# A hybrid mixer block on one core: scores a projection and a half apart, the next block's k projected behind them

## What is computed

```
h = rms_norm(x, ln_g);  proj = h @ w_in
scores = q @ k^T * 64**-0.5 + alibi, masked to the window of 128
p = softmax(concat(scores, sink))[:-1]
y_attn = (p @ v) * silu(g_attn)
```

## Time and profile before

| | us |
|---|---|
| median of 3 runs | 1454.54 |
| lowest, highest | 1451.94, 1455.07 |
| profiled execution, its own time | 1452.87 |
| its span, first to last instruction | 1450.7 |

### The profile page before, as it was taken

How to read it: one execution, slowest core, us unless ns; L and a number is a source line. 1 busy time by engine, 2 the same in 40 slices (tenths; PEclk the granted TensorE clock), 3 DMA queues, 4 the chain that set the end, 5 groups by cost and what they waited for, 6 DMA issues and landing times.

```text
span 1450.7 us, 20622 instructions
## 1 busy us (share of the span) xinstructions
PE 1363.4 (94%) x7070; PEld 1112.5 (77%) x7070; DVE 1170.9 (81%) x2365; ACT 549.3 (38%) x1421; POOL 504.8 (35%) x640
## 2 busy tenths in 40 slices
PE   6989898989989899876999999999999999999998
PEld 5867676767778687755888888888888888888886
DVE  4877768685868675554989999989899998888886
ACT  5746555555555554330221221121222243333332
POOL 5254545445354534552010010110101255555552
PEclk9999999999999999988999999999999999999999
DMA  9757482939384736657031230330326756545531
GB/s 214 218 125 263 124 284 89 288 110 268 124 254 153 203 146 162 245 130 222 12 131 54 108 131 24 136 130 14 131 88 250 286 193 213 164 158 163 159 126 73
DMA packets 112426, 230.78 MB, mean 159 GB/s; under 512 B 16464, under 2 KB 74192, under 8 KB 104656
## 3 DMA queue, kind: packets, MB, share of 16 engines
q1 hardware_dynamic: 88192, 205.85, 42.5%
q10 hardware_dynamic: 24144, 23.80, 6.8%
HBM read 131.05 MB, written 98.57 MB: 158 GB/s over the span
## 4 chain that ended last, share of the span: by engine, by line
PE 66%; DVE 14%; DMA 8%; ACT 5%; POOL 3%; issue 2%; SPq 1%; POOLq 0%; ACTq 0%; DVEq 0%
PE wide L346 12%; PE wide L347 12%; PE wide L348 12%; DMA xs<-in_x_dram 5%; PE pair L1239 3%; PE pair L1233 3%; PE pair L1234 3%; DVE m_tail L1994 3%; DVE a_rows L1038 2%; ACT a_rows L909 2%; PE wide L1233 2%; PE wide L1234 2%; PE turn L1202 2%; PE wide L1239 2%; PE turn L347 2%
## 5 line engine op out<-in xcount | busy, mean ns | idle before, releaser
L1994 DVE SCALAR_TENSOR_TENSOR m_tail<-m_tail,m_taps 128x512 f32<-128x512 f32 x480 | 338.5, 750 | 4.6
L1233 PE MATMUL pair<-xT,w_hi 128*128 128x512 f32 x384 | 154.5, 402 | 27.0 <-ACT xT L333 23.5
L845 POOL TENSOR_SCALAR a_rows<-a_rows,a_inv 128x128 f32<-128x128 f32 x256 | 108.4, 443 | 204.1 <-DVE a_inv L1058 204.0
L1736 POOL TENSOR_TENSOR operand_sums<-m_y 128x512 f32<-128x512 f32 x75 | 102.2, 1362 | 167.7 <-PE wide L348 116.6
L108 POOL TENSOR_TENSOR pool_carrier<-pool_carrier 128x1 f32<-128x1 f32 x23 | 14.0, 611 | 394.5 <-DVE m_meanvar L2003 394.5
L1234 PE MATMUL pair<-xT,w_lo 128*128 128x512 f32 x384 | 150.8, 393 | 0.0
L1239 PE MATMUL pair<-xT,w_hi 128*128 128x512 f32 x384 | 149.2, 394 | 0.9 <-DVE xT L339 0.7
L346 PE MATMUL wide<-x_first,w_hi 128*128 128x512 f32 x320 | 125.4, 392 | 0.0
L346 PE MATMUL wide<-xT,w_hi 128*128 128x512 f32 x320 | 125.2, 391 | 0.0
L348 PE MATMUL wide<-x_first,w_hi 128*128 128x512 f32 x320 | 124.6, 389 | 0.0
L348 PE MATMUL wide<-xT,w_hi 128*128 128x512 f32 x320 | 124.5, 389 | 0.0
(11 more groups left out here) (262 smaller groups left out, 3233.8 us busy)
## 6 DMA issues: line engine op xcount, KB each, us to landing
xT_scratch<-xT SPq DMA_DIRECT2D x16, 2048.0 KB, 10.3
p_scratch<-a_rows SPq DMA_DIRECT2D x32, 512.0 KB, 2.6
x_first<-xT_scratch SPq DMA_DIRECT2D x16, 1024.0 KB, 8.7
xT<-xT_scratch SPq DMA_DIRECT2D x16, 1024.0 KB, 9.0
combo_scratch<-stage SPq DMA_DIRECT2D x28, 512.0 KB, 5.3
m_y<-y_scratch ACTq DMA_DIRECT2D x14, 1024.0 KB, 6.6
xs<-in_x_dram SPq DMA_DIRECT2D x20, 512.0 KB, 10.7
a_pT<-p_scratch SPq DMA_DIRECT2D x64, 128.0 KB, 4.7
```

What stands on the lines that cost most here:

```text
L845: last = nc.gpsimd.tensor_scalar(probs[b][:, h], probs[b][:, h], inv[:, b, h:h + 1], 0.5, ALU.mult, ALU.mult)
L1233: nc.tensor.matmul(out, w.hi(c)[:, kk, cols], st.hi[:, kk, :], start=(kk == 0), stop=False)
L1736: nc.gpsimd.tensor_tensor(operand_sums[:, i, 1], y_block(q, left), y_block(q, right), SIGN[op]).then_inc(operand_sum, 1)
L1994: nc.vector.scalar_tensor_tensor(out=conv[:, i, :], in0=h[:, i, j:j + TB], scalar=taps[:, i, j:j + 1], in1=conv[:, i, :], op0=ALU.mult, op ...
```

## The change

- PE: k of block n+1 is projected at the end of block n, behind g3. attend(n-1, 0) comes first in the block, then q0 to q3 with the fold in q3. scores(0) follows q3 directly, then attend(n-1, 1) and v. scores(1), with `turn_v` in it, stands in the middle of g0, scores(2) behind g1, scores(3) in the middle of g3.
- q0 and q1 wait for one kv less of the last scores.
- ACT: the four `scale` steps move out of the q projections, in between the exponentials; `take_v` and the copy of the transposed v are placed anew; the four early `split_hi` come before both exponentials of subtile 3.
- DVE: the four `turn_squares` move between the subtiles, all four early `split_lo` come before `take_scores(3)`; `square_more` comes after q_lo(1), `mean` before q_lo(3), `output(n-1, 0)` and the transpose of the last probabilities right after k_lo.
- POOL: the masks of subtiles 2 and 3 come before `root`, the mask of subtile 0 behind `normalise(1)`, that of subtile 1 behind `normalise(2)`.
- SP: the next x is loaded first; the load of subtile 2 comes before the store of subtile 3.
- The last block has an order of its own on each engine.

The diff:

```diff
@@ -739,10 +739,10 @@
...
             else:
+                st.load(sp, n + 1, (0, 1))
+                load_probs(sp, n - 1, 2)
                 store_probs(sp, n - 1, 3)
-                st.load(sp, n + 1, (0, 1))
-                for j in (2, 3):
-                    load_probs(sp, n - 1, j)
+                load_probs(sp, n - 1, 3)
@@ -860,18 +860,14 @@
             if n == 0:
                 make_seen()
             else:
-                mask(n - 1, 1)
+                for j in (2, 3):
+                    mask(n - 1, j)
             if n < NB - 1:
                 st.root(pool, n + 1, carrier)
-            if n > 0:
-                for j in (2, 3):
-                    mask(n - 1, j)
             for j in range(SUB):
                 normalise(n, j)
-                if j == 2:
-                    mask(n, 0)
-                    if n == NB - 1:
-                        mask(n, 1)
+                if j in (1, 2):
+                    mask(n, j - 1)
@@ -946,63 +942,70 @@
...
-            elif not final:
+            q_hi(n, 1)
+            if not first and not final:
                 st.square(act, n + 1)
-            q_hi(n, 1)
...
             q_hi(n, 2)
-            if not first and not final:
-                st.scale(act, n + 1, 0)
...
-            else:
-                st.scale(act, n + 1, 1)
             q_hi(n, 3)
-            if not first and not final:
-                st.scale(act, n + 1, 2)
-            for s in combos.of_block(n, (3,)):
+            for s in combos.of_block(n, (3, 4)):
...
-            if first:
-                for part in (0, 1):
-                    st.scale(act, 1, part)
-            act.wait_ge(st.squared, SUB + st.HALF * (n if final else n + 1))
-            copy_out(n, slot("v"), vT)
-            for s in combos.of_block(n, (4,)):
-                combos.split_hi(act, s)
-            if not first and not final:
...
+            if not final:
+                st.scale(act, n + 1, 0)
+            for kv in range(KV):
+                exps(n, 0, kv)
+            take_v()
+            if not final:
+                st.scale(act, n + 1, 1)
+            for kv in range(KV):
+                exps(n, 1, kv)
+            spread_v()
+            gate_tanh(n, 0)
+            if not final:
+                st.scale(act, n + 1, 2)
+                gate_tanh(n, 1)
+                exps(n, 2, 0)
+                exps(n, 2, 1)
                 st.scale(act, n + 1, 3)
-            if first:
-                st.scale(act, 1, 2)
-            for j in range(SUB):
...
-                if j == SUB - 1 and not final:
-                    for kk in range(st.AHEAD):
...
-                if final and j == 2:
-                    w.split_hi(act, CHUNK_GP)
-                if j:
...
-                if j == 0:
-                    gate_tanh(n, j)
...
-                if j == 0:
-                    act.wait_ge(v_turned, n + 1)
...
+                gate_tanh(n, 2)
+                for kk in range(st.AHEAD):
+                    st.split_hi(act, n + 1, kk)
+                exps(n, 3, 0)
+                gate_tanh(n, 3)
+                exps(n, 3, 1)
@@ -1108,69 +1111,84 @@
...
+            make_k_lo(n)
             if not first:
+                output(dve, n - 1, 0)
                 turn_squares_of_probs(SUB * n - 1)
-            make_k_lo(n)
             make_q_lo(n, 0)
...
-            if not first:
-                output(dve, n - 1, 0)
-                if not final:
-                    st.square_more(dve, n + 1)
...
-                if t == 1 and not first and not final:
+                if t == 3 and not final:
                     st.mean(dve, n + 1)
                 make_q_lo(n, t)
-                if t == 3 and not first and not final:
-                    st.turn_squares(dve, n + 1, 1)
+                if t == 1 and not first and not final:
+                    st.square_more(dve, n + 1)
                 make_combos(n, (t,) if t < 3 else (3, 4))
...
-                elif t == 2 and not final:
-                    st.turn_squares(dve, n + 1, 0)
-                elif t == 3 and first:
-                    for part in (0, 1):
-                        st.turn_squares(dve, 1, part)
-                elif t == 3 and not final:
-                    st.turn_squares(dve, n + 1, 2)
...
+            take_scores(n, 0, 0)
+            take_scores(n, 0, 1)
             if not first:
                 output(dve, n - 1, 1)
-            for j in range(SUB):
-                take_scores(n, j, 0)
-                if j in (1, 2):
...
-                take_scores(n, j, 1)
-                invert(4 * n + j, j % 2, 0)
-                if j == 3:
-                    turn_squares_of_probs(SUB * n + 2)
-                if first and j < 2:
-                    st.turn_squares(dve, 1, 2 + j)
-                elif j == 0 and not first and not final:
...
-                if j == SUB - 1 and not final:
-                    st.split_lo(dve, n + 1, 0)
-                if j:
-                    gate_make(n, j)
-                if j == SUB - 1 and not final:
-                    for kk in range(1, PIECE):
-                        st.split_lo(dve, n + 1, kk)
-                invert(4 * n + j, j % 2, 1)
-                if j == 0:
-                    gate_make(n, j)
-                if final and j == 2:
...
+            inverts(0)
+            next_x(0)
+            take_scores(n, 1, 0)
+            turn_squares_of_probs(SUB * n)
+            take_scores(n, 1, 1)
+            next_x(1)
+            inverts(1)
+            gate_make(n, 0)
+            if not final:
+                next_x(2)
+                gate_make(n, 1)
+                take_scores(n, 2, 0)
+                turn_squares_of_probs(SUB * n + 1)
+                take_scores(n, 2, 1)
+                inverts(2)
+                next_x(3)
+                gate_make(n, 2)
+                for kk in range(PIECE):
+                    st.split_lo(dve, n + 1, kk)
+                for kv in range(KV):
+                    take_scores(n, 3, kv)
+                turn_squares_of_probs(SUB * n + 2)
+                gate_make(n, 3)
+                inverts(3)
@@ -1220,7 +1238,7 @@
...
             if name[0] == "q":
-                need(pe, score_taken, 2 * SUB * n)
+                need(pe, score_taken, 2 * SUB * n - (1 if name in ("q0", "q1") and n > 0 else 0))
@@ -1283,36 +1301,48 @@
...
+        def halfway(action):
+
+            return lambda kk: action() if kk == KT // 2 - 1 else None
+
...
                 project(n, "k", lambda kk: st.transpose(pe, kk + TURNS) if kk + TURNS < KT else None)
-                project(n, "q0")
             else:
-                project(n, "k")
-                project(n, "q0")
                 attend(pe, n - 1, 0)
-            final = isinstance(n, int) and n == NB - 1
-            for name in ("q1", "q2", "q3", "v"):
-                project(n, name, folding(n) if name == ("q3" if first else "q2") and not final else None)
+            for name in ("q0", "q1", "q2", "q3"):
+                project(n, name, folding(n) if name == "q3" and not final else None)
             pe.wait_ge(q_taken, GROUP * (n + 1))
+            scores(n, 0)
             if not first:
                 attend(pe, n - 1, 1)
...
-            for j in range(SUB):
-                scores(n, j, turn_v if j == 1 else None)
-                project(n, f"g{j}")
+            project(n, "v")
             if final:
+                scores(n, 1, lambda: turn_v(n))
...
                 attend(pe, n, 0)
+            else:
+                project(n, "g0", halfway(lambda: scores(n, 1, lambda: turn_v(n))))
+                project(n, "g1")
+                scores(n, 2)
+                project(n, "g2")
+                project(n, "g3", halfway(lambda: scores(n, 3)))
+                project(n + 1, "k")
```

## The result

The changed kernel takes **1540.36 us** (median of 4 runs, 1538.24 to 1541.36) against 1454.8 (median of 4, 1451.94 to 1455.7). The ratio is **1.059**, 95% interval 1.0571 to 1.0608: 5.9% slower, +85.6 us. The forecast was 1498, with 1526 as the range's upper end, so the sign was right and the size was half of what came. The profiled execution has a span of 1537.9 us (before: 1450.7).

The account below looks back on a forecast made before the run. PE sets the pace, save where a DVE and ACT chain ends later. Middle blocks +6.1 six times (+36.6), block 0 +10.3, block 7 -3: +43.9 on 1452.87 gives 1496.8, median 1498 us; range 1460 to 1526.

Parts of the forecast that it names:

- A + 37.5: Fifth split_hi ready 37.5 us after the start of scores(1) (A = 0); PE wanted it at 26.8.
- The new wait at scores(0): PE waits some 2.2 us at each block's first scores until all of q3 is rounded, eight times.
- The front: Block's stretch from the end of k (T = 0) to the start of scores(1): 41.1 us in a middle block.
- I take 1.2: Delay of DVE's squares of the next x by the masks of subtile 3: 1.2 us, at most some 3.5.
- The tail: Block's stretch from the start of scores(1) to the end of the next k: 42.5 us.
- the upper end, 3.8: Most that the mask of subtile 1 could add to the four early split_lo; 2.0 us was taken.
- Block 0: First block: k ends at 105.5 against 95.2 before, +10.3 us.
- Block 7: Last block, no next x: scores(1) at 44 us after the end of k instead of 47.4; -3 us together.
- The third: Rival: squares and split_lo pay whole mask passes, 3.5 and 3.8 us; 87.7 a block, 1524 us; chance 0.18.
- The mild rival: POOL's masks miss the tail's DVE and ACT chain, squares are in time: 78.4 a block, 1463 us; chance 0.17.
- The faster rival: DVE's chain is hidden, fifth split_hi in time, PE loses only the q wait: 70.0 a block, 1403 us; chance 0.10.

Follow-up runs that it names:

- masks23_small: The changed kernel with GpSimd's mask passes of subtiles 2 and 3 cut to one head of eight (work left out): 1500.02 us, ratio 1.0322.
- masks01_small: The changed kernel with GpSimd's mask passes of subtiles 0 and 1 cut to one head of eight (work left out): 1502.17 us, ratio 1.0319.
- filler_all: The changed kernel with useless matmuls on PE: 40 ahead of k's fifth slice, 10 ahead of the fold, 8 ahead of the wait for q: 1520.76 us.
- filler_k: The changed kernel with 40 useless matmuls on PE ahead of the fifth slice of every k but the first: 1524.52 us, ratio 1.048.

## Why the prediction was right or wrong

**Direction: right**, by the mechanism named. PE waits for ACT's xT once a block, 10.5 us (forecast 8 to 10, some 60 in all; 72.6 measured; the sum itself had 37.5 - 26.8 = 10.7). The fifth split_hi is written at A + 38.3 (A = 155.89; 194.16 on ACT), forecast A + 37.5. The new wait at scores(0) is there eight times, 2.1 us in a middle block (forecast 2.2). negmax in take(2, 0) takes 1.03.

**The front, 41.1 forecast, 47.0 measured: wrong.** The step that failed is the squares, "I take 1.2". They start at T + 16.2 and end at T + 23.9, 4.9 us later than their 2.8 undisturbed, more than the 3.5 that I gave as the most: five squares met a pass; four lost 1.1 us each and the first 0.6. PE thus waited 3.2 at the fold, where the statement was that it waits under 2, and where the sum had 1.2. (That sum was loose in itself: it gave PE 1.3 to spare at the fold and still charged the squares' delay of 1.2 in full.) The second part of that step was never written: having cleared the fold, I priced no slow clock in the front at all, though the earlier trace rows showed it behind a wait of 2.7 us. It costs 3.4 a block, and is the larger part: of the 5.9 us missed, 3.4 are slow clock, 2.0 the wait and 0.5 the rest. With the squares in time (`masks23_small`) the front is 40.4, within the forecast's 39.9 to 41.1, so all the rest of that sum held.

**The tail, 42.5 forecast, 44.4 measured: the right mechanism, undersized.** The splits grew by 3.9, not 2.0: the upper end, 3.8, was the value to take. take(2, 0) grew by 0.9, not by 2.0, since only negmax met a pass. Behind the wait PE's 15 matmuls took 6.05 us instead of the 5.0 assumed: at 0.50 of the clock for 3.5 us, and the last of them not yet back at full. These are the stretches from 183.7 on:

```profile
183.70:194.20 10.50, 0.04 (x1) 0.00 (x0) 10.17 (x31) 4.44 (x21) 3.53 (x4) 0.59 0.04 15
194.20:197.70 3.50, 3.42 (x8) 2.75 (x9) 3.08 (x4) 1.87 (x4) 3.50 (x6) 0.50 0.25 104
```

**Block 0: +13.7, forecast +10.3.** The wait for q was 3.82 us there and the one of k 10.26. **Block 7: -6.7, forecast -3**: its scores(1) stand at T + 40.4 (694.18) and not T + 44, of which 2.4 are the masks that I expected it to wait 5.0 for, and which cost it 2.6; the other 1.2 I can't place:

```profile
685.57 1.09 PE L1220 MATMUL turn<-a_pT,a_v 128*64 128x128 f32 x16 [2.59 <-POOL a_rows L856]
...
753.96 1.97 PE L1220 MATMUL turn<-a_pT,a_v 128*64 128x128 f32 x16 [16.49 <-POOL a_rows L856]
```

In sum 13.7 + 79.7 - 6.7 = +86.7, of a span that grew by 87.2. Where block 1 stands for the six, 35 us of the missed time are the front's and 11 the tail's (the mean block is 0.6 us shorter than it), block 0 adds 3 and block 7 takes 4 off.

**The rivals.** The third (full blocking, 1524) came nearest, and its mechanism is what happened; it fell short by the front's slow clock, 3.4 a block. Its 3.5 us for the squares were too few for the squares (4.9), but about the wait that came of them (3.2), since PE had time to spare. The rule of the Trainium skill beside it (SBUF: State Buffer, Who interferes with whom), that the second of two such instructions blocks fully, agrees with this trace: 1.50 us a square (the kernel gives it x as both of its inputs) beside passes of 1.35 to 1.47, 0.41 without. I gave it 0.18, because the trace of before had no such row for squares, and took a value near the low end of each bound instead. The row that I took for the nearest, four splits against a normalise made of four short instructions, was a poor proxy: there it was POOL that grew, from 1.42 to 3.12 us. And the trace of before has nearer rows, which I overlooked: an operation of the combos, 128x512 with both inputs in SBUF like the splits, takes 0.69 us undisturbed and 1.59 in block 1 when a pass of a mask has begun just before it (1.51 and 1.35 in two other places). DVE, and POOL beside it, in the kernel before:

```profile
121.26 1.59 DVE L500 TENSOR_TENSOR stage<-raw,stage 128x512 fp32r<-128x512 f32 x1 [1.49 <-ACT stage L496]
```

```profile
121.01 1.29 POOL L856 TENSOR_TENSOR a_pT<-a_pT,a_rows 64x512 f32<-64x512 f32 x1
```

At 0.9 us a meeting, an estimate from this row, four splits lose 3.6 us; 3.9 came. So the third rival's price for the splits was the one to take. The mild rival, 1463, was not measured as such: no run leaves out all the masks in the changed order. If the gains of `masks23_small` and `masks01_small` simply added, 40.3 and 38.2 us, it would be 1462, an estimate. The faster rival (1403) would have needed DVE's chain 10.7 us shorter; of the contention only 4.8 a block (3.9 and 0.9) stand in that chain, and none of the runs got below the kernel before in the new layout. The SP part of the change, which I did not price on its own, is worth -17 by itself in the kernel before.

## What to carry to other kernels

Where VectorE has dense stretches, lay GpSimd's long passes against its timeline first: a run of back-to-back passes costs each small VectorE instruction that it meets most of a pass (here 0.9 to 1.1 us of 1.3), so count the meetings in instructions, not in us, and take the upper bound where both are packed. Look for the slow clock behind every wait of PE of the size that had it in a trace (here 2.7 us in the kernel before, 2.1 in the changed one and in `filler_all`), in the front as well as at the largest wait; but count it as gained only where PE's busy time falls too. And a load that others wait for belongs ahead of a store in the queue: that one exchange was worth 17 us here, while moving a mask or a rounding only passed the wait on, to whoever stood next behind it.

## What the runs showed of the hardware that was not expected

- VectorE instructions of three sizes were held until the GpSimd pass beside them had ended: 4 columns (negmax, with one tensor as input, 0.17 to 1.03 us), 256 (a square, 0.41 to 1.50), 512 (four split_lo, 2.8 to 6.72). The passes grew too, but less (from 1.26 to 1.29 us to 1.35 to 1.47 beside the squares, and to 1.73 beside the splits).
- The same wait of 2.10 us, at the first scores, left the clock at 1.00 in `masks23_small` (135.65 to 148.79) and went with 0.88 in the changed kernel (141.28 to 155.89), where the fold had waited 3.18 us shortly before and q3 had run in part at the lower level. Why only there was not tried apart.
- Matmuls without use, in a wait that is there anyway, give back the slow clock behind it (-16 us for seven waits of 10.5 us), if they last nearly to its end: 2.13 us left idle were enough for q3 to run as slowly as without them, while 1.49 us left idle at k (192.39 in `filler_k`) went with a clock of 1.00 behind it.
